# One joint pass of the PEER query projection for the last two prompt tiles and the sample, wider gather rings, and another order on TensorE

## What is computed

```python
def peer(xn, w_q, sub_keys, u_tab, v_tab):
    q = (xn @ w_q).reshape(t, PEER_HEADS, 2, PEER_HALF)          # 8 heads, 2 halves of 128
    s = einsum('thpc,pnc->thpn', q, sub_keys)                     # scores against 2 x 128 keys
    top_s, top_i = top_k(s, 16)                                   # the 16 best of each half
    cand_s = top_s[:, :, 0, :, None] + top_s[:, :, 1, None, :]    # their sums
    cand_e = top_i[:, :, 0, :, None] * 128 + top_i[:, :, 1, None, :]
    best_s, best_j = top_k(cand_s, 16)                            # 16 experts of each head
    experts = take_along_axis(cand_e, best_j); gates = softmax(best_s)
    # per row: 128 rows of u_tab and 128 rows of v_tab, 1024 floats each
    act = gelu(einsum('cd,ced->ce', xb, take(u_tab, eb)))
    out = einsum('ce,ced->cd', gb * act, take(v_tab, eb))
```

## Time and profile before

| | before |
|---|---|
| runs, median (lowest to highest) | 2011.76 us (2002.02 to 2023.05) |
| the profiled execution | 2029.6 us |
| TensorE busy, MATMUL records | 1467.7 us (72%), 5470 |
| VectorE busy | 1202.8 us (59%) |
| GpSimd busy | 1067.7 us (53%) |
| ScalarE busy | 380.8 us (19%) |
| DMA, mean over the span | 348 GB/s |
| of it gathers and copies by GpSimd's queue | 612.40 MB |

### The profile page before, as it was taken

How to read it: one execution, slowest core, us unless ns; L and a number is a source line. 1 busy time by engine, 2 the same in 40 slices (tenths; PEclk the granted TensorE clock), 3 DMA queues, 4 the chain that set the end, 5 groups by cost and what they waited for, 6 DMA issues and landing times.

```text
span 2029.6 us, 18882 instructions
## 1 busy us (share of the span) xinstructions
PE 1467.7 (72%) x5470; PEld 670.5 (33%) x5470; DVE 1202.8 (59%) x3335; ACT 380.8 (19%) x923; POOL 1067.7 (53%) x1082
## 2 busy tenths in 40 slices
PE   8999998756886687768996555555555666676657
PEld 5444443443443333322442222222222233221111
DVE  1034352585577567667666776677676777687541
ACT  2113441222222222111111111211111212111101
POOL 3020000264575566766566666666666666666674
PEclk9999999976897888778997877777777777776778
DMA  9999998697999799999999989999999999998997
GB/s 329 359 310 365 362 318 304 199 323 260 389 388 362 274 375 343 396 397 375 396 364 403 376 332 344 342 365 361 368 352 368 347 352 357 354 361 332 369 369 284
DMA packets 226136, 706.43 MB, mean 348 GB/s; under 512 B 21153, under 2 KB 46657, under 8 KB 226009
## 3 DMA queue, kind: packets, MB, share of 16 engines
q0 software_dynamic: 166912, 612.40, 80.5%
q1 hardware_dynamic: 59120, 92.82, 13.2%
HBM read 700.65 MB, written 72.61 MB: 381 GB/s over the span
## 4 chain that ended last, share of the span: by engine, by line
PE 26%; DVE 23%; issue 19%; DMA 11%; POOL 9%; another core or an unknown queue 8%; ACT 1%; SPq 1%; DVEq 0%; POOLq 0%; ACTq 0%
PE bank L1059 7%; PE bank L947 4%; DVE XS L1463 4%; POOL WR L660 4%; DVE GT L1463 3%; DMA arena<-in_peer_u_dram,e_all 3%; PE bank L1175 3%; POOL XS L660 2%; DMA WR<-in_peer_v_dram,arena 2%; DVE arena L1463 2%; PE bank L1076 2%; PE bank L1196 2%; PE bank L1154 2%; DMA WR<-in_w_in_dram 2%
## 5 line engine op out<-in xcount | busy, mean ns | idle before, releaser
L1059 PE MATMUL bank<-WR,arena 128*64 128x512 f32 x1728 | 536.1, 724 | 189.8 <-issue 82.1
L660 POOL DMA_INDIRECT WR<-in_peer_v_dram,arena x432 | 427.0, 988 | 301.0 <-issue 145.4
L660 POOL DMA_INDIRECT XS<-in_peer_u_dram,e_all x258 | 269.2, 1043 | 225.7 <-DVE XS L1463 77.4
L1059 PEld LDWEIGHTS bank<-WR,arena 128*64 128x64 f32 x1728 | 146.8, 163 | 520.2 <-issue 470.2
L1463 DVE SCALAR_TENSOR_TENSOR XS<-XS,bank 128x1024 f32<-128x1024 f32 x144 | 171.2, 1218 | 41.3 <-DMA XS<-in_peer_u_dram,e_all 38.8
L1463 DVE SCALAR_TENSOR_TENSOR GT<-GT,bank 128x1024 f32<-128x1024 f32 x126 | 150.0, 1218 | 59.8 <-DMA GT<-in_peer_u_dram,e_all 45.3
L1463 DVE SCALAR_TENSOR_TENSOR XS<-XS,GT 128x1024 f32<-128x1024 f32 x114 | 137.4, 1225 | 80.1 <-DMA XS<-in_peer_u_dram,e_all 65.6
L660 POOL DMA_INDIRECT GT<-in_peer_u_dram,e_all x126 | 123.1, 977 | 52.3 <-issue 33.9
L660 POOL DMA_INDIRECT arena<-in_peer_u_dram,e_all x128 | 127.4, 995 | 42.1 <-issue 37.8
L754 ACT ACTIVATE XS<-bank 128x256 f32<-128x256 f32 (+1 forms) x90 | 36.2, 405 | 469.1 <-remote 267.7
L1076 PE MATMUL bank<-WR,XS 128*128 128x512 f32 x256 | 116.0, 607 | 0.4 <-ACT arena L754 0.4
(11 more groups left out here) (234 smaller groups left out, 2122.9 us busy)
## 6 DMA issues: line engine op xcount, KB each, us to landing
out_dram<-in_cache_a_k_dram POOLq DMA_DIRECT2D x8, 4064.0 KB, 54.6
out_dram<-in_cache_a_v_dram POOLq DMA_DIRECT2D x8, 4064.0 KB, 55.4
WR<-in_w_in_dram SPq DMA_DIRECT2D x8, 2048.0 KB, 25.7
GT<-in_w_peer_q_dram SPq DMA_DIRECT2D x14, 1024.0 KB
WR<-in_w_out_dram SPq DMA_DIRECT2D x6, 2048.0 KB
WR<-in_peer_v_dram,arena POOLq DMA_INDIRECT x432
WR<-in_w_branch_a_dram SPq DMA_DIRECT2D x6, 1024.0 KB, 7.6
WR<-in_w_branch_b_dram SPq DMA_DIRECT2D x6, 1024.0 KB, 9.7
```

The costliest lines, as they stand in the source:

```text
L660: nc.gpsimd.indirect_dma_start(dst, None, table, bass.IndirectOffsetOnAxis(ap=idx, axis=0))\
L1059: last = nc.tensor.matmul(b[c][R * j:R * j + R, :], diag[p // QUAD % 4][:, s % 4, :], V[V_AT[s]][:, c * CHUNK:(c + 1) * CHUNK], start=Fals ...
```

## The change

Three edits. First, the queries of tiles 2, 3 and the sample are made in one pass: for each of eight heads 16 matmuls with 264 moving columns (128 + 128 + 8) take the place of three times 16 with 128 (JOINT = 2). The queries of tile 3 and the sample are kept on chip (q_later) until their scores are due. The normed rows of all three must be ready before, so tile 2's heads start at place 55 and not 51; tile 3's scores start at 76 and not 75. w_pq now has two places, filled in turn, and a block that is still there from the pass before is used again (block_of rotates the order), so tile 1 loads 7 blocks and the joint pass 6: 21 blocks in all, as before.

Second, the space that w_pq had goes to the rings: U has 12 places from quad 80, V has 12 from quad 56 and 16 from quad 78, diag has 6 from quad 60. Four of the sample's broadcast rows (hbc) have a place instead of eight; rows 4 to 7 are made at place 124 and wait for DVE's use of rows 0 to 3.

Third, from place 51 on tensor_order() puts the quad first on TensorE.

```diff
+JOINT = 2
+COLS = 2 * P + DEC
+def block_of(t, h):
+    return (h + (0, PH - 1, PH - 3)[t]) % PH
+def query_buffer(t, h):
+    return 1 if (t, h) == (1, PH - 2) or t == JOINT and h % 2 == 0 else 0
 def head_at(t, h):
-    return SLOT0 + {1: 20, 2: 51, 3: 75, SAMPLE: 99}[t] + {1: 4, SAMPLE: 2}.get(t, 3) * h
+    return SLOT0 + {1: 20, 2: 55, 3: 76, SAMPLE: 99}[t] + {1: 4, SAMPLE: 2}.get(t, 3) * h
 ...
-        put(head_at(SAMPLE, PH - 1) + 1 + b, "rows", b)
+        put(head_at(SAMPLE, PH - 1) + 1 + b if b < DEC // 2 else SLOT0 + SQ, "rows", b)
 ...
+AFTER_MIXES = SLOT0 + 51
+def tensor_order(x, pieces, beside):
+    if x >= AFTER_MIXES:
+        return sorted(pieces, key=lambda p: 0 if p[0] == "quad" else 1)
 ...
-UR, VR = 8, 12
-WIDER_U, WIDER_V, WIDEST_V = 44 * QUAD, 56 * QUAD, 80 * QUAD
+UR, VR = 12, 16
+U_AT, U_FILL, U_OLD = ring(TILES * SLOTS + DEC, {0: 4, 44 * QUAD: 8, 80 * QUAD: UR})
+V_AT, V_FILL, V_OLD = ring(TILES * SLOTS + DEC, {0: 8, 56 * QUAD: 12, 78 * QUAD: VR})
+D_AT, _, D_OLD = ring(TILES * TILE_Q, {0: 4, 60: 6})
 ...
+                elif U_AT[s] >= 8:
+                    filled(pool, "query", JOINT, PH - 1, 1)
 ...
                     elif stage == "rows":
-                        filled(act, "query", SAMPLE, PH - 1, 0)
+                        if at[0] >= HBC:
+                            act.wait_ge(S["u_used"], S0 + at[0] - HBC + 1)
 ...
                         for c in range(2):
+                            if t == JOINT and c == 1:
+                                b, landed = take("query", t, h, 1)
                             for k in range(KO):
-                                last = nc.tensor.matmul(b[:, c * P:(c + 1) * P], weights[:, c * P:(c + 1) * P], hnT[:, k, :],
+                                out, rows = (b[:, c * P:(c + 1) * P], hnT[:, k, :]) if t < JOINT else (b[:, 0:COLS], hn_joint[:, k, :])
+                                last = nc.tensor.matmul(out, w_q[i][:, k, c * P:(c + 1) * P], rows,
                                                         start=(k == 0), stop=(k == KO - 1))
 ...
-                if v >= 4:
-                    dve.wait_ge(S["v_used"], (asked(QUAD * (v - 3) - 1) + 1) // G)
-                V_.tensor_tensor(diag[v % 4], ...
+                if D_OLD[v] is not None:
+                    dve.wait_ge(S["v_used"], (asked(QUAD * (D_OLD[v] + 1) - 1) + 1) // G)
+                V_.tensor_tensor(diag[D_AT[v]], ...
```

More of the change, by code:

```diff
@@ L64, in asked_q, with query_loads @@
     return asked(p * QUAD) // QUAD
+JOINT = 2
+COLS = 2 * P + DEC
+LATER = {3: slice(0, P), SAMPLE: slice(P, P + DEC)}
+def block_of(t, h):
+    return (h + (0, PH - 1, PH - 3)[t]) % PH
+def query_buffer(t, h):
+    return 1 if (t, h) == (1, PH - 2) or t == JOINT and h % 2 == 0 else 0
+QUERIES = [(t, h) for t in range(JOINT + 1) for h in range(PH)]
+def query_loads():
+    loads, held, count, user = {}, [None, None], [0, 0], [None, None]
+    for t, h in QUERIES:
+        b = query_buffer(t, h)
+        new = held[b] != block_of(t, h)
+        count[b] += new
+        loads[t, h] = (b, count[b], user[b] if new else None, new)
+        held[b], user[b] = block_of(t, h), (t, h)
+    return loads
+QUERY_LOADS = query_loads()
 HELD_FROM = {t: max(t * TILE_Q, 38) for t in range(1, TILES)}
@@ L186, in tensor_order @@
         two = sum(p[0] == "att" for p in rest) == 2
-        rest.sort(key=lambda p: 2 if p[0] == "quad" else 1 if two and p[0] == "att" else 0)
+        rest.sort(key=lambda p: 3 if p[0] == "rows" and p[1] >= DEC // 2 else 2 if p[0] == "quad" else 1 if two and p[0] == "att" else 0)
     return head + rest
@@ L219 @@
     for _piece in _pieces:
-        for _j in range(USES.get(_piece[0], 0)):
+        for _j in range(uses_of(_piece)):
             MISC[_piece + (_j,)] = len(MISC)
@@ L225, with ring @@
 MIX_ORDER = {t: i for i, t in enumerate((0, 1, 2, SAMPLE, 3))}
-def ring(slots, buffers):
-    where, filled, before, last = [], [], [], {}
+def ring(slots, sizes):
+    order, where, filled, before, last = [], [], [], [], {}
     for s in range(slots):
-        b = buffers(s)
+        if s in sizes:
+            order = list(range(len(order), sizes[s])) + order
+        b = order.pop(0)
+        order.append(b)
         where.append(b)
@@ L405, in hybrid_step_kernel @@
         u_landed = [sem(f"u_landed{j}") for j in range(UR)]
-        wq_in = [sem(f"wq_in{h}") for h in range(PH)]
+        wq_in = [sem(f"wq_in{b}") for b in range(2)]
         x_again_in = [sem(f"x_again{t}") for t in range(ALL)]
@@ L621, in _ @@
             x_again(3)
[L622 to L627 removed]
+            for h in range(PH):
+                query_weights(JOINT, h)
             answer(1)
@@ L1179, in _ @@
                         t = at[0]
+                        n = P if t < TILES else DEC
                         pe.wait_ge(S["hn"], t + 1)
-                        transposes(hidden[t][:, 0:CHUNK], 4, "hidden", t, 0)
-                        transposes(hidden[t][:, CHUNK:D], 4, "hidden", t, 1)
+                        for half in range(2):
+                            b, landed = take("hidden", t, half)
+                            for k in range(4):
+                                col = (4 * half + k) * P
+                                last = nc.tensor.transpose(b[:, k * P:k * P + n], hidden[t][0:n, col:col + P], ident[0:n, 0:n])
+                            last.then_inc(landed, 1)
@@ L1580, in _ @@
                             V_.tensor_copy(dst[:, :], b[:, 0:DEC]).then_inc(S["tT"], 1)
+                        dve.wait_ge(S["tT"], 2)
+                        for i in range(2):
+                            dve.sem_inc(free[misc_bank("sample_turn_lists", i)], 1)
                     elif stage == "finish" and at[1] == 1:
```

159 lines of the change are left out of this document (82 added, 77 removed).

## The result

In 14 runs each, taken in turn on the same chips, the kernel before took 2022.3 us (median) and the changed one 2035.6 us; the ratio is 1.0082, interval [1.0058, 1.0106]. So it is slower by about 13 to 17 us, within the 1% that the prediction called no change, but on the wrong side: 1998 was forecast, and the range ended at 2028. Of the 37.6 us between 1998 and 2035.6, 10.5 belong to the base: 2011.76 was the median of three runs, and with the 14 it is 2022.3. The other 27 are the change itself, forecast at -14 and measured at +13. The trace of the changed kernel has a span of 2033.9 us, from a run of 2035.92, at the median. The one of before has 2029.6, more than any of its 14 runs took. So the two traces differ by 4.3 us only, and I compare stretches and not whole spans.

A forecast was written before the change was run, and what follows sets the result against it. Gathers were taken to bound the kernel, held back by GpSimd's stops. Wider rings -17 us and the joint pass +3 gave -14: 2015.6 on the profiled 2029.6, so runs at 1998 us; 8-in-10 range 1960 to 2028.

The forecast's parts named there:

- What bounds the kernel: From 450 us on the gathers set the pace; GpSimd's stops cost 46 and 75 us in two stretches.
- Quads 56 to 79: Sign that the joint pass was judged rightly: this stretch takes 280 to 292 us; over 300 meant TensorE late.
- The split, -4.6 for V and +3 for TensorE: Quads 56 to 77: V's 10 to 12 places win 4.6 us; denser TensorE work in joint heads costs 3 us.
- The wide rings: From quad 80, four more U and V places win 0.25 us a quad, 11 us, plus 1.5 in the last six.
- The sign that I named for being right: From quad 80 gathers go from 1.478 to about 1.447 us each, with stops after three quads rather than two.
- TensorE's given-back time: The joint pass gives back about 90 to 150 us of TensorE's time; counted as no gain for the kernel.
- the third rival: TensorE's given-back time is what freed v places late: about -45 to -60 us, 1951 to 1967 us; chance 0.20.
- the 40 that were forecast: Sign of being right: TensorE's busy time falls by 40 us or more at no like gain in the span.
- The first rival: Data rate is fixed; wider rings make fewer, longer stops: 2012 us; mark 355 GB/s, stops 7 us or more; chance 0.22.
- The page that I weighed: Skill section "Where 436 GB/s comes from": one core's HBM share about 358 GB/s binds, so time would stay as it is.

The follow-up runs named there:

- e13: Kernel before, with one of eight products kept in each half of tile 3's and the sample's query heads: ratio 0.9989 to the kernel before.
- e1: Changed kernel with U kept at 8 places and V at 12 to the end: ratio 1.0141 to the kernel before.
- e5: Changed kernel with U 8 and V 12 places and the old order on TensorE, no added work: ratio 1.015 to the kernel before.
- e9: As e5, plus sixteen unused 128-column products ahead of the score in each head of tile 3 and the sample: ratio 1.0048 to the kernel before.
- e4: Changed kernel, GpSimd waiting before each gather so that at most three are under way: ratio 1.209 to the kernel before.
- e8: Changed kernel, GpSimd waiting before each gather so that at most four are under way: ratio 1.0465 to the kernel before.
- e14: Changed kernel with U 12, V 12; before every second gather GpSimd waits for the landing of the fourth before it: ratio 1.0391 to the kernel before.
- e15: Changed kernel with U 12, V 12; at every eighth gather GpSimd waits for the landing of the fourth before it: ratio 1.0101 to the kernel before.
- e2: Changed kernel with V kept at 12 places, U at 12 from quad 80: ratio 0.9964 to the kernel before.
- e16: The same code as e2, measured again: ratio 1.0012 to the kernel before.

## Where the prediction was right and where wrong

**What bounds the kernel: right.** The gathers do, and what is lost is lost in GpSimd's stops.

**Quads 56 to 79: right.** 280 to 292 us was the mark, and 279.9 came, at its lower end; TensorE isn't late with the joint heads. A head takes 7.39 us at a granted clock of 1.00, as worked out (7.4); two of the eight had stretches of lower clock, the longest took 14.3 us from first to last.

```profile
1170.54 7.39 PE L1244 MATMUL bank<-arena,PP 128*128 128x264 f32 x32
```

The split, -4.6 for V and +3 for TensorE, isn't shown: the stretch is 8.9 us shorter in this trace, and traces of one code differ by 6. e13 has the code of before in nearly all of it and took 281.8 us there, so even the 8.9 can't be put down to the change.

**The wide rings, -12.5 us from quad 80 on: about right in sum, wrong in its parts.** From e1 to the changed kernel is -0.6%, 12 us, with an interval about as wide. But I sized it as a V ring's, since the earlier trace rows name VectorE with 14.3 us and the unnamed v stops with 57.9. The rows were of a kernel with TensorE's queries in it. In the changed kernel U is what stops GpSimd: U's four places give 1.3 to 1.8% with twelve v places, and V's last four take 0.7 to 1.2%. The sign that I named for being right, 1.447 us a gather from quad 80 on, didn't come either: it is 539.0 / 352 = 1.531, with the stops after three quads.

**TensorE's given-back time, counted at nothing: this is the step that failed.** Everything in the change but the wide rings costs 1.4 to 1.5% (e1, e5), 28 to 31 us, where the sum had +3; giving the work back returns 0.7 to 1.0%, 15 to 21 us, of it. The rest, some 10 to 15 us, has no shown cause, and since e13 loses nothing by the same relief, the work costs time only together with something else of the change. I argued that TensorE isn't what GpSimd waits for, so that its time can't matter, and in the third rival that it could only help. In e9 an engine that is off the path still set at which ring GpSimd stopped, and the stop that comes otherwise depends on VectorE, which in the changed kernel was busy 1.08 of 11.70 us while the queues were full. TensorE's busy time fell by 69 us (1467.7 to 1398.5), over the 40 that were forecast.

**The first rival had half of the mechanism.** "Fewer and longer stops" is what came: 7.2 us after three quads where it was 5.6 after two, and its mark, 355 GB/s or less and stops of 7 us, is met with 344. It wasn't carried through: a longer stop doesn't only work off a backlog, it leaves the queues dry. In quads 80 to 103 the DMA engines were busy 0.94 x 281.1 = 264 us before and 0.89 x 294.7 = 262 us after, so by these shares all of the 13.6 us is idle time of theirs. What was wrong in that rival was its reason, a rate that is what it is, and that it had no way to a time over 2012.

**The page that I weighed.** The stretch from 1105.2 to 1394.0 us moves 384 GB/s over 288.8 us, one core at work, so a limit of about 358 doesn't hold here. The Trainium skill, "DMA: Bandwidth & Descriptors", section "Measured (HBM→SBUF, 128 partitions, SWDGE, issued from GpSimd)", says itself that the half share of about 358 GB/s is for both cores of a pair streaming; this trace agrees with that, and I had used only the other section.

## What to carry to other kernels

Before a ring is widened or an engine relieved, ask which stop comes next and who ends it. Here the dear stop was the one that needed an engine which stood still under full queues. Time taken from an engine off the path may move the stop to another ring: adding it back made this kernel faster (e9), though taking it from the kernel before did no harm (e13). So such a relief isn't to be costed at nothing without naming the next stop. And a ring's gain read from one step of it (V from 10 to 12) holds for the mix of waits in which it was read, and for no other.

## What the runs showed of the hardware

VectorE's long waits on its own results came only in the kernels that had five or more gathers of 512 KB under way for longer than a moment: in quads 80 to 123 there is none over 1.5 us with three or four (e4, e8) and none in e14, 3 in e15, 19 and 28 with five, and 16 to 26 in the kernels without a cap that are in the table, 1.5 to 9 us each. Why VectorE stands so long at a semaphore that it raises itself, no view shows. The Trainium skill, "Trainium Architecture — The Big Picture", section "What this means for kernel authors", says that engine lanes and DMA ports of the SBUF can't contend; VectorE's instructions themselves keep their length (a u product takes 1.22 us in the changed kernel as with a cap of three), only the waits between them grow, which agrees as far as it goes.

Two traces of one code differ by 6 us in a stretch of 280, and the medians of one code against the same kernel by 0.5% (e2, e16).
